# Attention stage of a decoder step: cached products in four stretches, three buffers of probabilities, 128-wide transposes of the new tokens, page numbers read ahead

## The chip, the core and the metric

The kernel runs on one core of a Trainium2 chip (trn2). The core has TensorE (PE in the profile; its weight loads are PEld), VectorE (DVE), ScalarE (ACT), GpSimd (POOL) and SyncE (SP), which in this kernel issues the transfers. The metric is the time of one execution in microseconds on the device, the median of several runs; lower is better.

## The reference

One inference step of a two-layer decoder trunk, for a prompt of 256 tokens and for 8 sequences that each get 8 new tokens after 256 cached ones. The first layer mixes with an mLSTM, the second with attention over shared keys and values; both have a half feed-forward network ahead and behind. What matters here is the attention of the second layer (D 1024, 8 heads of 128):

```python
q = (h @ w_q_b[j]).reshape(bt, t, B_HEADS, B_HD)
att = moba_attention(q, k_all, v_all, q_pos, q_block)
out = att.reshape(bt, t, B_HW) @ w_out_b[j]
...
s = jnp.einsum('bqhd,bqhnkd->bqhnk', qf, kg.astype(F32)) * scale
s = s - slopes[None, None, :, None, None] * dist.astype(F32)
s = jnp.where(ok[..., None] & (dist >= 0), s, -jnp.inf)
p = jax.nn.softmax(s.reshape(bt, q_block, nh, -1), axis=-1).reshape(s.shape)
out = jnp.einsum('bqhnk,bqhnkd->bqhd', p, vg.astype(F32))
```

For the prompt `k_all` and `v_all` are its own 256 tokens. For the 8 sequences they are two pages of 128 cached tokens each, found in a pool by `page_table`, and the 8 new tokens behind them.

## The kernel before

Activations lie transposed, 320 token columns wide (256 of the prompt, 64 new). A product with a weight matrix is a run of "units" of 2 x 8 blocks; each block is three passes (lines 556 to 558) over a high and a low part of weights and activations. ACT and DVE split the raw weights into those parts two units ahead of PE, and SP loads raw weights into a ring of four slots (`raw`). Attention stands between the unit run of the queries (U_Q, four units) and that of the output projection (U_OB, four units).

There is no scheduler: every engine runs a list written out by hand and waits on semaphores. In the attention stage the lists hold these steps (S, T and so on are my short names):

- S(h), `prompt_scores`, lines 954 and 955: scores of head h of the prompt, 128 + 256 columns. DVE adds the position bias and takes maxima (`prompt_bias`, lines 2122 and 2127) into the buffer `pp`, which lies in the room `work`, ACT takes the exponential (`prompt_exp`, line 1538), DVE divides by the sum (`prompt_probs`, lines 2132 and 2134).
- T(h), `prompt_turn`, line 965: three transposes of the probabilities. ACT copies them to `pt` (`prompt_copy`, line 1545).
- O(h), `prompt_outputs`, lines 975 and 976: probabilities times values. ACT and DVE keep the high and low part (`prompt_hi` 1549, `prompt_lo` 2140), which free the output bank for O(h + 1).
- C(b), `cache_scores`, lines 1001 and 1007: for sequence b, the scores of all heads against both cached pages. Each matmul gives 32 rows, and four of them run beside each other in four column groups (form 128*32 in the trace). `new_scores`, line 984, does the same for the new tokens.
- N(i) and P(i), `turn_new_probs` (1018) and `turn_page_probs` (1024): transposes of the probabilities `ss` of four sequences and four heads, for the new tokens and for the two pages. DVE spreads them (`spread_probs`, 2157 to 2162).
- V(b), `cache_outputs`, line 1059: probabilities times cached values, four column groups again; `new_outputs`, line 1037, is the part of the new tokens. Sequences 0 to 3 go to bank 4, 4 to 7 to banks 0 and 2.
- the rows of the sequences are turned in `turn_early_outputs` (1070) and `turn_late_outputs` (1081).

Pages are "cache units": 0 to 7 are the keys of the eight sequences, 8 to 15 their values, each of two pages of 512 KB. Units 4 to 8 and 13 to 15 go to rooms of their own, the others to the ring; the rooms of 13, 14 and 15 are those of the keys 4, 5 and 6, so their loads wait until these keys are used (`kv_used`). For each page SP reads the number from `pages` and then issues the transfer (`page_of`, `load_cache`, `load_room`, lines 493 to 509). Units 7 and up are issued once the last query unit is multiplied.

Of the kernel before, what the change touches and what calls it, by code (L numbers as in the profile page):

```python
# [26 lines left out]
H = 8  # L27
# [42 lines left out]
def trunk_program(nc, w_in, w_out, w_a, w_oa, w_kv, w_q, w_ob, w_gate, xp_in, con_in, row_in,  # L70
# [6 lines left out]
    with ctx:  # L77
# [30 lines left out]
        pp = work[:, 0:768].rearrange("p (s k) -> p s k", s=2)  # L108
        pt = work[:, 768:1536].rearrange("p (s k) -> p s k", s=2)
# [14 lines left out]
        with ExitStack() as ov:  # L124
# [35 lines left out]
            with ExitStack() as own:  # L160
# [6 lines left out]
                ss = sb("ss", [128, 4, PAST + SLOT], f32, own)  # L167
                o_rows = sb("o_rows", [128, 4, DV], f32, own)
                page_k = sb("page_k", [128, 2048], f32, own)
                st = sb("st", [128, 2, 6], f32, own)  # L170
# [226 lines left out]
        def prompt_score_bank(h):  # L397

            return bank[{1: 6, H - 1: 1}.get(h, 5)]
# [31 lines left out]
        def _(sp):  # L431
# [60 lines left out]
            sp.wait_ge(s_pg, 16)  # L492
            def page_of(c, j):

                at = NPG * (c % NB) + j
                page = sp.value_load(pages[0:1, at:at + 1], min_val=0, max_val=kc_in.shape[0] - 1)
                return (kc_in if c < NB else vc_in)[bass.ds(page, 1), :, :].rearrange("a p c -> p (a c)")
# [55 lines left out]
        def _(pe):  # L553
# [404 lines left out]
            def prompt_turn(h):  # L958
# [5 lines left out]
                for i in range(3):  # L964
                    mm = pe.transpose(bank[6][:, i * 128:i * 128 + 128],
                                      pp[:, h % 2, i * 128:i * 128 + 128], ident)
# [46 lines left out]
            def turn_new_probs(i):  # L1013
# [3 lines left out]
                w = SLOT * (r % 2) + SLOT  # L1017
                pe.transpose(bank[r][0:w, 256:384], ss[:, r, PAST + SLOT - w:PAST + SLOT], ident)
# [65 lines left out]
            pe.wait_ge(x_ready, 4 * KT)  # L1084
            prompt_scores(0)
            prompt_scores(1)
            new_scores(0)
# [7 lines left out]
            cache_scores(0, (1,))  # L1095

            def cache_unit(c):

                if c < NB:
                    cache_scores(c)  # L1100
                else:
                    cache_outputs(c - NB)

            cache_unit(1)

            prompt_scores(2)
            prompt_turn(0)
            cache_unit(2)
            cache_unit(3)
            pe.wait_ge(qa_sp, 4)  # L1110
            cache_unit(4)

            prompt_outputs(0)
            prompt_scores(3)
            prompt_turn(1)
            cache_unit(5)
            cache_unit(6)
            cache_unit(7)

            turn_new_probs(0)  # L1120
            turn_page_probs(0)
            prompt_scores(4)
            prompt_turn(2)
            prompt_outputs(1)
            turn_new_probs(1)
            turn_new_probs(2)
            prompt_scores(5)
            turn_page_probs(1)
            turn_page_probs(2)
            prompt_outputs(2)  # L1130
            prompt_turn(3)
# [3 lines left out]

            turn_new_probs(3)
            turn_page_probs(3)
            prompt_outputs(3)
            prompt_turn(4)
            prompt_scores(6)  # L1140
            prompt_scores(7)
            prompt_turn(5)
            prompt_outputs(4)
            new_outputs(1)
            for c in range(NB + 4, NB + 7):
                cache_unit(c)

            prompt_turn(6)
            prompt_outputs(5)
            turn_early_outputs()  # L1150
# [4 lines left out]
            turn_late_outputs(0)  # L1155
            prompt_outputs(7)
            turn_late_outputs(1)
# [49 lines left out]
        def _(sc):  # L1207
# [447 lines left out]
        def _(ve):  # L1655
# [806 lines left out]
```

## Time and profile before

| | |
|---|---|
| median of 3 runs | 1240.37 us (1240.34 to 1240.64) |
| the profiled execution | 1240.44 us |
| its span | 1238.6 us |
| PE busy | 1233.2 us (100%), 8875 matmuls |
| PEld, DVE, ACT, POOL busy | 1210.4, 726.1, 582.7, 81.1 us |
| PE clock granted | 9 in each of 40 slices (90% or more) |
| DMA | 200.39 MB, mean 162 GB/s |
| attention stage | 936.8 to 969.1 us of the span |

The 1.8 us between the profiled time and its span lie outside the instructions and are taken as fixed.
### The profile page before, as it was taken

To read this page: it belongs to the slowest core of one execution; us is meant where nothing else is said; L and a number is where in the kernel's file an instruction comes from. 1 tells how busy PE (TensorE), PEld (TensorE's weight loads), DVE (VectorE), ACT (ScalarE), POOL (GpSimd) and SP (SyncE) were. 2 spreads that over 40 slices of the span, in tenths; PEclk is the share of its full clock that TensorE was granted. 3 is DMA by queue.
4 is the path that set the end of the run, shared out by engine and by line. 5 is a ranking of instruction groups with operands and counts; after the bars stand their busy time and mean duration, and the time that the engine had idled before them with its cause. 6 is when DMAs were issued, how large, how long until landed. Compare 5 with 4: busy or idle time off the path is not lost.

```text
span 1238.6 us, 22056 instructions
## 1 busy us (share of the span) xinstructions
PE 1233.2 (100%) x8875; PEld 1210.4 (98%) x8875; DVE 726.1 (59%) x1127; ACT 582.7 (47%) x936; POOL 81.1 (7%) x99
## 2 busy tenths in 40 slices
PE   9999999999999999999999999999999999999998
PEld 9999999989999999999998999999998999999998
DVE  7656554575777656555564565655467585565443
ACT  6534333464556445443345554534344474544343
POOL 0000000100332000000000000000020110000010
PEclk9999999999999999999999999999999999999999
DMA  8344334543354443334543734334478734433341
GB/s 341 137 161 144 112 132 155 205 147 131 127 164 147 157 166 137 134 121 140 187 166 137 262 136 151 143 105 153 163 277 317 287 139 142 163 135 127 125 156 43
DMA packets 34778, 200.39 MB, mean 162 GB/s; under 512 B 4050, under 2 KB 4186, under 8 KB 19490
## 3 DMA queue, kind: packets, MB, share of 16 engines
q1 hardware_dynamic: 32706, 192.24, 44.0%
q0 software_dynamic: 2016, 7.39, 1.9%
q8 instruction: 38, 0.62, 0.2%
q14 instruction: 18, 0.15, 0.0%
HBM read 193.03 MB, written 6.57 MB: 161 GB/s over the span
## 4 chain that ended last, share of the span: by engine, by line
PE 99%; DMA 0%; SPq 0%; DVE 0%; ACT 0%; issue 0%; DVEq 0%
PE bank L556 30%; PE bank L558 30%; PE bank L557 29%; PE bank L714 1%; PE bank L713 1%; PE bank L712 1%; PE bank L716 1%; PE bank L715 1%; PE bank L1059 1%; DMA xp<-xp_in 0%; PE bank L867 0%; PE bank L822 0%; PE bank L975 0%; PE bank L1001 0%; PE bank L1007 0%; PE bank L955 0%
## 5 line engine op out<-in xcount | busy, mean ns | idle before, releaser
L556 PE MATMUL bank<-h_hi,w_hi 128*128 128x320 f32 x1792 | 555.6, 310 | 0.5 <-DVE h_lo L1682 0.5
L558 PE MATMUL bank<-h_hi,w_lo 128*128 128x320 f32 x1792 | 553.8, 309 | 0.0
L557 PE MATMUL bank<-h_lo,w_hi 128*128 128x320 f32 x1792 | 553.7, 309 | 0.0
L1222 ACT ACTIVATE w_hi<-raw 128x1024 fp32r<-128x1024 f32 (+1 forms) x364 | 331.7, 958 | 440.7 <-PE bank L558 421.7
L1668 DVE TENSOR_TENSOR w_lo<-raw,w_hi 128x1024 fp32r<-128x1024 f32 (+1 forms) x364 | 388.5, 1108 | 133.1 <-ACT w_hi L1222 133.0
L556 PEld LDWEIGHTS bank<-h_hi,w_hi 128*128 128x128 f32 x1792 | 336.3, 188 | 2.6 <-issue 1.4
L557 PEld LDWEIGHTS bank<-h_lo,w_hi 128*128 128x128 f32 x1792 | 336.4, 188 | 0.1
L558 PEld LDWEIGHTS bank<-h_hi,w_lo 128*128 128x128 f32 x1792 | 336.3, 188 | 0.0
L557 PE MATMUL bank<-f_lo,w_hi 128*128 128x320 f32 x704 | 216.5, 308 | 0.0
L558 PE MATMUL bank<-f_hi,w_lo 128*128 128x320 f32 x704 | 216.5, 308 | 0.0
L556 PE MATMUL bank<-f_hi,w_hi 128*128 128x320 f32 x704 | 216.5, 308 | 0.0
L1711 DVE TENSOR_TENSOR work<-bank,rms 128x320 f32<-128x320 f32 x88 | 43.2, 491 | 152.0 <-PE bank L558 151.5
L558 PEld LDWEIGHTS bank<-f_hi,w_lo 128*128 128x128 f32 x704 | 131.9, 187 | 0.0
L556 PEld LDWEIGHTS bank<-f_hi,w_hi 128*128 128x128 f32 x704 | 131.9, 187 | 0.0
L557 PEld LDWEIGHTS bank<-f_lo,w_hi 128*128 128x128 f32 x704 | 131.9, 187 | 0.0
L1272 ACT ACTIVATE f_hi<-work 128x320 f32 (+1 forms) x88 | 41.5, 472 | 124.0 <-DVE work L1719 124.0
L1726 DVE TENSOR_TENSOR f_lo<-work,f_hi 128x320 f32 (+1 forms) x88 | 43.3, 492 | 64.5 <-ACT f_hi L1272 64.5
L2281 POOL TENSOR_TENSOR norm_room<-norm_room 128x320 f32<-128x320 f32 x41 | 43.8, 1068 | 264.9 <-ACT norm_room L1244 263.7
L1731 DVE SCALAR_TENSOR_TENSOR xp<-bank,xp 128x320 f32<-128x320 f32 x31 | 15.3, 493 | 67.3 <-PE bank L558 67.3
L2278 POOL COPY norm_room<-norm_room 128x320 f32<-128x320 f32 x6 | 5.0, 836 | 723.1 <-ACT norm_room L1244 723.1
L1682 DVE SCALAR_TENSOR_TENSOR h_lo<-xp,h_hi 128x320 fp32r<-128x320 f32 x56 | 44.8, 833 | 3.4 <-ACT h_hi L1247 3.4
L1719 DVE TENSOR_TENSOR work<-work 128x320 f32<-128x320 f32 x88 | 42.8, 486 | 4.8 <-ACT work L1268 4.8
(263 smaller groups left out, 763.0 us busy)
## 6 DMA issues: line engine op xcount, KB each, us to landing
raw<-w_in SPq DMA_DIRECT2D x86, 1024.0 KB, 4.8
raw<-w_out SPq DMA_DIRECT2D x64, 704.0 KB, 4.0
raw<-w_a SPq DMA_DIRECT2D x12, 1024.0 KB, 4.7
raw<-w_kv SPq DMA_DIRECT2D x8, 1024.0 KB, 4.7
raw<-w_oa SPq DMA_DIRECT2D x4, 1024.0 KB, 6.0
raw<-w_q SPq DMA_DIRECT2D x4, 1024.0 KB, 4.7
raw<-w_ob SPq DMA_DIRECT2D x4, 1024.0 KB, 11.8
raw<-kc_in SPq DMA_DIRECT2D x8, 512.0 KB, 4.5
```

The costliest lines, as they stand in the source:

```text
L556: pe.matmul(out, wh, mh, start=first, stop=False)
L557: pe.matmul(out, wh, ml, start=False, stop=False)
L558: return pe.matmul(out, wl, mh, start=False, stop=last)
L1222: sc.activation(w_hi[:, n_at % 2, part * w:part * w + w], raw[:, raw_of(n_at) % RAW, part * w:part * w + w], ACT.Copy).then_inc(hi_done, 1)
L1272: sc.activation(dst, up[:, k_at % 2, :], ACT.Copy).then_inc(hid_hi, 1)
L1668: ins = ve.tensor_tensor(w_lo[:, n_at % 2, c], raw[:, raw_of(n_at) % RAW, c], w_hi[:, n_at % 2, c].bitcast(f32), ALU.subtract)
L1682: ve.scalar_tensor_tensor(out=h_lo[:, m, :], in0=x[:, m, :], scalar=par[:, P_G + KT * norm + m:P_G + KT * norm + m + 1], in1=h_hi[:, m, :] ...
L1711: ve.tensor_tensor(gate[:, k_at % 2, :], bank[b][:, 0:T], rms[:, :], ALU.mult).then_inc(gate_ready, 1)
L1719: ve.tensor_tensor(up[:, k_at % 2, :], up[:, k_at % 2, :], act[:, k_at % 2, :], ALU.mult).then_inc(hid_ready, 1)
L1726: ve.tensor_tensor(lo, up[:, k_at % 2, :], hi.bitcast(f32), ALU.subtract).then_inc(hid_lo, 1)
L1731: ve.scalar_tensor_tensor(out=x[:, m, :], in0=bank[4 + m % 2][:, 0:T], scalar=0.5, in1=x[:, m, :], op0=ALU.mult, op1=ALU.add).then_inc(x_r ...
L2281: gp.tensor_tensor(sqsum[:, :], sqsum[:, :], sq[:, m % 2, :], ALU.add).then_inc(sum_done, 1)
```

## The change

The lists of PE, ACT and DVE in the attention stage are written in another order, and four things change beside:

1. The cached products (C and V) stand in four stretches: units 0 to 6; 7, the new tokens' part and 8 to 11; 12 to 14; 15. Prompt steps that stood between them go behind or ahead.
2. `pp` and `st` have three buffers instead of two, in the same room `work`, and the scores of heads 2 and 4 go to bank 4. S(2) is issued at the start; bias and exponential of head h wait for head h - 3 and no longer for h - 2. `new_outputs(0)`, which writes bank 4, waits until head 4 is biased (`pr_b` 5).
3. `turn_new_probs` transposes a full width of 128 instead of 32 or 64. `ss` is wider by 96 columns for that, which POOL sets to zero once, long before.
4. The page numbers of units 7 to 13 are read by `read_pages` during the query units, ahead of units 1, 2 and 3's loads. `page_of` also reads both numbers of any other unit before its first page is issued.

```diff
-        pp = work[:, 0:768].rearrange("p (s k) -> p s k", s=2)
-        pt = work[:, 768:1536].rearrange("p (s k) -> p s k", s=2)
+        pp = work[:, 0:1152].rearrange("p (s k) -> p s k", s=3)
+        pt = work[:, 1152:1920].rearrange("p (s k) -> p s k", s=2)
...
-            return bank[{1: 6, H - 1: 1}.get(h, 5)]
+            return bank[{1: 6, 2: 4, 4: 4, H - 1: 1}.get(h, 5)]
...
+            def read_pages(units):
+
+                for c in units:
+                    for j in range(NPG):
+                        at = NPG * (c % NB) + j
+                        page_read[c, j] = sp.value_load(pages[0:1, at:at + 1], min_val=0,
+                                                        max_val=kc_in.shape[0] - 1)
...
             load_room(6, 1)
+            read_pages((7,))
             load_cache(1)
+            read_pages((NB, NB + 1, NB + 2))
             load_cache(2)
+            read_pages((NB + 3, NB + 4, NB + 5))
             load_cache(3)
...
+            BIASED_BEFORE = {3: 1, 4: 3, 5: 4, 6: 6}
+
             def prompt_scores(h):
-                if 2 <= h < H - 1:
-                    pe.wait_ge(pr_b, h if h > 2 else 1)
+                if h in BIASED_BEFORE:
+                    pe.wait_ge(pr_b, BIASED_BEFORE[h])
...
-                w = SLOT * (r % 2) + SLOT
-                pe.transpose(bank[r][0:w, 256:384], ss[:, r, PAST + SLOT - w:PAST + SLOT], ident)
+                at = PAST - SLOT * (r % 2)
+                pe.transpose(bank[r][:, 256:384], ss[:, r, at:at + 128], ident)
...
                 pe.wait_ge(sm_tc, 6 * q + 6)
+                if q == 0:
+                    pe.wait_ge(pr_b, 5)
...
-                if h >= 2:
-                    sc.wait_ge(pr_p, h - 1)
+                if h >= 3:
+                    sc.wait_ge(pr_p, h - 2)
...
-                if h >= 2:
-                    ve.wait_ge(pr_t, h - 1)
+                if h >= 3:
+                    ve.wait_ge(pr_t, h - 2)
...
+            gp.memset(ss[:, :, PAST + SLOT:PAST + 128], 0.0).then_inc(spread_set, 1)
```

The new list of PE, in the short names, from the first scores on ("new" is `new_scores`, "n-out" `new_outputs`; strokes bound the stretches of four-column-group work):

```
before: S0 S1 | new C0 C1 | S2 T0 | C2 C3 C4 | O0 S3 T1 | C5 C6 C7 | N0 P0 S4 T2 O1 N1 N2 S5 P1 P2 O2 T3 |
        n-out0 V0..V3 | N3 P3 O3 T4 S6 S7 T5 O4 | n-out1 V4 V5 V6 | T6 O5 early | V7 | T7 O6 late0 O7 late1
after:  S0 S1 S2 | new C0..C6 | T0 S3 N0 P0 T1 O0 S4 N1 T2 S5 P1 O1 | C7 n-out0 V0..V3 |
        T3 O2 N2 S6 P2 T4 N3 O3 early P3 S7 T5 O4 | n-out1 V4 V5 V6 | O5 T6 | V7 | T7 O6 late0 late1 O7
```

The new list of DVE after the bias of heads 0, 1 and 2 and the first two `sample_bias` is: probs 2, bias 3, spread 0, lo 0, bias 4, spread 1, bias 5, sample bias 2, probs 3, probs 4, sample bias 3, lo 1, lo 2, spread 2, probs 5, lo 3, spread 3, bias 6, bias 7 and so on; before, it was bias 3, lo 0, probs 2, sample bias 2, probs 3, bias 4, lo 1, spread 0, spread 1, sample bias 3, bias 5, lo 2, probs 4, spread 2, probs 5, spread 3, lo 3, bias 6, bias 7.

First place, PE at the first cached products. Before, the rows from S(1) on (x4 to x16 are matmuls of 32 rows; the first two rows are the scores of head 1):

```order
L954 MATMUL bank<-k_all,qa 128x128
L955 MATMUL bank<-k_all,qa 128x256
L984 MATMUL bank<-k_all,qa 32x32 x8
L1007 MATMUL bank<-raw,q_spread 32x256 x4
L984 MATMUL bank<-k_all,qa 32x32 x8
L1007 MATMUL bank<-raw,q_spread 32x256 x12
L954 MATMUL bank<-k_all,qa 128x128
L955 MATMUL bank<-k_all,qa 128x256
L965 MATMUL bank<-con,work 128x128 x3
L1007 MATMUL bank<-raw,q_spread 32x256 x16
```

After the change (line numbers are those of the changed kernel; the first two rows are S(2)):

```order
L969 MATMUL bank<-k_all,qa 128x128
L970 MATMUL bank<-k_all,qa 128x256
L999 MATMUL bank<-k_all,qa 32x32 x8
L1022 MATMUL bank<-raw,q_spread 32x256 x4
L999 MATMUL bank<-k_all,qa 32x32 x8
L1022 MATMUL bank<-raw,q_spread 32x256 x28
L1016 MATMUL bank<-page_k,q_spread 32x128 x16
L1016 MATMUL bank<-keys_room,q_spread 32x128 x16
L1016 MATMUL bank<-row_room,q_spread 32x128 x4
L1016 MATMUL bank<-norm_room,q_spread 32x128 x4
L1016 MATMUL bank<-row_room,q_spread 32x128 x4
L1016 MATMUL bank<-norm_room,q_spread 32x128 x4
```

The scores of head 2 stand ahead, the turn of head 0 (`bank<-con,work`) is gone from between the products, and key units 4, 5 and 6 (`page_k`, `keys_room`, `row_room` with `norm_room`) follow the ring's units at once.

Second place, PE from the key unit 7 (`split_room<-q_spread`) on. Before:

```order
L1001 MATMUL bank<-split_room,q_spread 32x128 x16
L1018 MATMUL bank<-con,ss 32x128
L1024 MATMUL bank<-con,ss 128x128 x2
L954 MATMUL bank<-k_all,qa 128x128
L955 MATMUL bank<-k_all,qa 128x256
L965 MATMUL bank<-con,work 128x128 x3
L975 MATMUL bank<-work,v_tok 128x256
L976 MATMUL bank<-work,v_tok 128x128
L1018 MATMUL bank<-con,ss 32x128
L1018 MATMUL bank<-con,ss 64x128
```

After:

```order
L991 MATMUL bank<-work,v_tok 128x128
L1016 MATMUL bank<-split_room,q_spread 32x128 x16
L1054 MATMUL bank<-v_tok,p_new 32x128 x8
L1076 MATMUL bank<-split_room,p_spread 32x128 x16
L1076 MATMUL bank<-raw,p_spread 32x128 x48
L980 MATMUL bank<-con,work 128x128 x3
L990 MATMUL bank<-work,v_tok 128x256
```

Unit 7 stood ahead of the first transposes; it now stands next to the new tokens' values (`v_tok,p_new`) and the value units 8 to 11, and the transposes of `ss` come before it.

Third place, SP at the pages of unit 7. Before, from its first transfer on (`TENSOR_LOAD pages` reads a page number, ISA are register instructions):

```order
L509 DMA split_room<-kc_in 128x1024
L496 TENSOR_LOAD pages
L496 ISA x2
L509 ISA
L509 DMA split_room<-kc_in 128x1024
L496 TENSOR_LOAD pages
L496 ISA x2
```

After, from the last reads ahead of unit 3's loads on:

```order
L500 TENSOR_LOAD pages
L500 ISA x2
L500 TENSOR_LOAD pages
L500 ISA x2
L514 ISA
L514 DMA raw<-kc_in 128x1024
L514 ISA
L514 DMA raw<-kc_in 128x1024
L519 ISA
L519 DMA split_room<-kc_in 128x1024
L519 ISA
```

Each transfer of unit 7 and on stood behind a read of its own; now they follow each other, and the reads stand ahead of unit 3.

## Rows read from the trace of the kernel before

**Rows 1.** Timeline of PE: start, duration, line, form; stage's first and last.
```profile
936.80 0.38 PE L954 MATMUL bank<-k_all,qa 128*128 128x128 f32 x2
...
969.08 0.38 PE L556 MATMUL bank<-h_hi,w_hi 128*128 128x320 f32 x1
```

**Rows 2.** The same timeline: steps at edges of stretches and between.
```profile
937.46 0.38 PE L954 MATMUL bank<-k_all,qa 128*128 128x128 f32 x2
...
940.32 0.49 PE L954 MATMUL bank<-k_all,qa 128*128 128x128 f32 x2
...
941.19 0.55 PE L965 MATMUL bank<-con,work 128*128 128x128 f32 x3
941.67 1.93 PE L1007 MATMUL bank<-raw,q_spread 128*32 128x256 f32 x32
...
950.98 0.38 PE L1018 MATMUL bank<-con,ss 128*32 128x128 f32 x2
951.32 0.49 PE L954 MATMUL bank<-k_all,qa 128*128 128x128 f32 x2
...
952.07 0.60 PE L1024 MATMUL bank<-con,ss 128*128 128x128 f32 x4
...
960.31 0.49 PE L965 MATMUL bank<-con,work 128*128 128x128 f32 x3
960.63 0.60 PE L975 MATMUL bank<-work,v_tok 128*128 128x256 f32 x2
...
961.38 0.65 PE L1037 MATMUL bank<-v_tok,p_new 128*32 128x128 f32 x16
...
962.72 1.06 PE L1059 MATMUL bank<-page_k,p_spread 128*32 128x128 f32 x32
963.59 1.06 PE L1059 MATMUL bank<-keys_room,p_spread 128*32 128x128 f32 x32
964.58 0.55 PE L965 MATMUL bank<-con,work 128*128 128x128 f32 x3
```

**Rows 3.** Waits of PE's weight loads, 930 to 985 us (total, times, longest).
```profile
PEld bank L965 <- DVE work L2134: 0.3, 1, 0.3
```

**Rows 4.** Timeline of SP's queue: transfers issued (units 1, 3, 7, 15; w_ob).
```profile
922.75 0.34 SPq L504 DMA_DIRECT2D raw<-kc_in  x1
...
935.32 0.34 SPq L504 DMA_DIRECT2D raw<-kc_in  x1
...
937.71 1.44 SPq L509 DMA_DIRECT2D split_room<-kc_in  x2
...
957.33 0.34 SPq L509 DMA_DIRECT2D norm_room<-vc_in  x1
...
957.71 0.91 SPq L443 DMA_DIRECT2D raw<-w_ob  x2
```

**Rows 5.** DMA issues at 935.32, 937.71 and 957.33: KB, us to landing.
```profile
raw<-kc_in SPq DMA_DIRECT2D x1, 512.0 KB, 5.0
...
split_room<-kc_in SPq DMA_DIRECT2D x1, 512.0 KB, 4.6
...
norm_room<-vc_in SPq DMA_DIRECT2D x1, 512.0 KB, 8.4
```

**Rows 6.** Busy time in a window (PE, PEld, DVE, ACT, POOL), clock, DMA, GB/s.
```profile
950.00:955.00 5.00, 5.00 (x77) 4.40 (x79) 4.86 (x20) 3.03 (x11) 0.00 (x0) 1.00 1.03 415
```

**Rows 7.** Timeline of PE: start of the last cached product, V(7).
```profile
965.93 0.43 PE L1059 MATMUL bank<-row_room,p_spread 128*32 128x128 f32 x8
```

**Rows 8.** Timeline of DVE: bias of head 3, spread 2, lo 3.
```profile
946.42 0.56 DVE L2122 SCALAR_TENSOR_TENSOR work<-con,bank 128x384 f32<-128x384 f32 x1 [0.84 <-PE bank L965]
...
956.45 0.48 DVE L2157 COPY p_spread<-bank 128x128 f32<-128x128 f32 x2
...
959.28 0.42 DVE L2140 TENSOR_TENSOR h_lo<-bank,h_hi 128x256 fp32r<-128x256 f32 x1
```

More of the change, by code:

```diff
@@ L492, in _ @@
             sp.wait_ge(s_pg, 16)
+            page_read = {}
+            def read_pages(units):
[4 more added lines that the diff above has]
+                                                        max_val=kc_in.shape[0] - 1)
             def page_of(c, j):
-                at = NPG * (c % NB) + j
-                page = sp.value_load(pages[0:1, at:at + 1], min_val=0, max_val=kc_in.shape[0] - 1)
-                return (kc_in if c < NB else vc_in)[bass.ds(page, 1), :, :].rearrange("a p c -> p (a c)")
+                if (c, j) not in page_read:
+                    read_pages((c,))
+                return (kc_in if c < NB else vc_in)[bass.ds(page_read[c, j], 1), :, :].rearrange("a p c -> p (a c)")
             def load_cache(c):
@@ L1084, in _, with cache_unit @@
             pe.wait_ge(x_ready, 4 * KT)
+            def cache_unit(c):
+                if c < NB:
+                    cache_scores(c)
+                else:
+                    cache_outputs(c - NB)
             prompt_scores(0)
             prompt_scores(1)
+            prompt_scores(2)
             new_scores(0)
@@ L1095, in _ @@
             cache_scores(0, (1,))
[L1097 to L1106, printed above, removed]
-            prompt_turn(0)
[L1108 to L1113, printed above, removed]
+            for c in range(1, 4):
+                cache_unit(c)
+            pe.wait_ge(qa_sp, 4)
+            for c in range(4, 7):
+                cache_unit(c)
+            prompt_turn(0)
             prompt_scores(3)
[L1115 to L1118, printed above, removed]
             turn_new_probs(0)
             turn_page_probs(0)
+            prompt_turn(1)
+            prompt_outputs(0)
             prompt_scores(4)
+            turn_new_probs(1)
             prompt_turn(2)
-            prompt_outputs(1)
-            turn_new_probs(1)
-            turn_new_probs(2)
             prompt_scores(5)
             turn_page_probs(1)
-            turn_page_probs(2)
-            prompt_outputs(2)
-            prompt_turn(3)
+            prompt_outputs(1)
+            cache_unit(7)
             new_outputs(0)
@@ L1134, in _ @@
                 cache_unit(c)
+            prompt_turn(3)
+            prompt_outputs(2)
+            turn_new_probs(2)
+            prompt_scores(6)
+            turn_page_probs(2)
+            prompt_turn(4)
             turn_new_probs(3)
+            prompt_outputs(3)
+            turn_early_outputs()
             turn_page_probs(3)
-            prompt_outputs(3)
-            prompt_turn(4)
-            prompt_scores(6)
             prompt_scores(7)
@@ L1553, in sample_exp @@
                 sc.wait_ge(sm_m, i + 1)
-                sc.activation(ss[:, r, :], ss[:, r, :], ACT.Exp, bias=sst[:, 0, r:r + 1],
+                sc.activation(ss[:, r, 0:PAST + SLOT], ss[:, r, 0:PAST + SLOT], ACT.Exp, bias=sst[:, 0, r:r + 1],
                               accum_out=sst[:, 1, r:r + 1]).then_inc(sm_e, 1)
@@ L1570, in late_hi @@
                               ACT.Copy).then_inc(sm_hi, 1)
-            prompt_exp(0)
-            prompt_exp(1)
-            prompt_copy(0)
-            prompt_exp(2)
+            for h in range(3):
+                prompt_exp(h)
             sample_exp(0)
             sample_exp(1)
+            prompt_copy(0)
+            prompt_copy(1)
             prompt_hi(0)
             prompt_exp(3)
-            prompt_copy(1)
-            sample_exp(2)
+            prompt_exp(4)
             prompt_hi(1)
             prompt_copy(2)
-            prompt_hi(2)
-            prompt_copy(3)
-            prompt_exp(4)
+            sample_exp(2)
             sample_exp(3)
-            prompt_exp(5)
-            prompt_hi(3)
-            prompt_copy(4)
             sc.wait_ge(kv_used, NB + 4)
@@ L1593, in _ @@
             sample_rows(0, bank[4][:, 0:DV])
+            prompt_copy(3)
+            prompt_hi(2)
             sample_rows(2, bank[4][:, DV:2 * DV])
+            prompt_exp(5)
+            prompt_copy(4)
+            prompt_hi(3)
+            early_hi()
+            prompt_hi(4)
+            prompt_copy(5)
             prompt_exp(6)
-            prompt_hi(4)
             prompt_exp(7)
-            prompt_copy(5)
+            prompt_hi(5)
             prompt_copy(6)
-            early_hi()
-            prompt_hi(5)
             sc.wait_ge(sm_og, 1)
@@ L1606, in _ @@
             late_hi(0)
+            prompt_hi(6)
             late_hi(1)
-            prompt_hi(6)
             prompt_hi(7)
```

51 lines of the change are left out of this document (25 added, 26 removed).

## Prediction

> **What bounds the kernel now.** I first read the busy shares on the page: PE is busy for 1233.2 of 1238.6 us, so nothing that DVE, ACT or SP saves counts by itself; only what shortens PE's own list, or a wait of PE, does. The change touches PE's list in the attention stage alone, so I went to PE's timeline there. The first scores start at 936.80 and the first pass of the output projection at 969.08 [rows 1]: the stage takes 32.28 us, 2.6% of the time. The whole can only move by what moves in it. Then the waits of PE in the stage: only one that another engine causes is above 0.2 us, T0 behind DVE's probabilities [rows 3]. So the stage is not held up by waits; what it holds beside its bare products is the edges between kinds of work.
>
> Bare steps, from start to start [rows 1, 2]: S takes 0.66 (936.80 to 937.46), and O, with the same 384 columns, the same; T takes 0.32 (960.31 to 960.63); a cached product V 0.87 (962.72 to 963.59). A transpose of 128 columns is a third of a T, 0.11. With 8 S, 8 O, 8 T, 16 C or V, 16 single transposes (N, P, early, late) and some 1.2 for the new tokens' parts, the bare sum is 10.6 + 2.6 + 13.9 + 1.8 + 1.2 = 30.1. The stage has 2.2 us over that, and no reordering of it can give back more: 0.18% of 1240. Below I count changes within 0.2% (2.5 us), about what a measurement of this kernel can tell from no change, as the same.
>
> Second in line is the stream of pages. Over 950 to 955 the DMA engines are full (share 1.03, 415 GB/s) at a granted clock of 1.00 [rows 6], the upper one of PE's levels, 2.4 GHz. The last page is issued at 957.33 and lands 8.4 later, at 965.73 [rows 4, 5]; V7, which needs it, starts at 965.93 [rows 7]. So the stream ends 0.2 us ahead of its use: whatever PE saves ahead of V7 is lost there unless the pages come earlier too. This decides what the reordering is worth.
>
> **The change part by part.**
>
> *Two stretches fewer.* I count six stretches of four-column-group work before and four after (the change's own words say seven). An edge costs, on entering: O4 takes 0.75 (960.63 to 961.38) instead of 0.66, so 0.09. On leaving: V6 takes 0.99 (963.59 to 964.58) instead of 0.87, so 0.12, and leaving C1 is dearer: S2 behind it takes 0.87 (940.32 to 941.19) instead of 0.66, with T0's wait at its end. T0 ahead of C2 takes 0.48 (941.19 to 941.67) instead of 0.32, 0.16 [rows 2]. For two stretches I take the mean of entering, 0.12, and 0.17 for leaving: 2 x 0.29 = 0.58, from 0.42 (both at the low rows) to 0.7.
> By the Trainium skill, TensorEngine Tiling (Array Packing), Tiling Modes, a change of the tiling mode drains the array, and TensorE: Matmul & The Clock Gate gives that drain as 128 cycles, which is 0.053 us at 2.4 GHz: by that, four edges would give 0.21, an estimate; the rows of this trace say more than twice that.
>
> *128-wide transposes.* N1 and N2 take 0.34 together (950.98 to 951.32) instead of 0.22, and S5 behind them 0.75 (951.32 to 952.07) instead of 0.66 [rows 2]: they are edges of the same kind, 0.21 in sum. N0 stands beside a stretch and N3 alone; I count nothing for them. In the new order all are full width between full-width steps: 0.21 saved. The wider `ss` costs POOL one memset during the query units, where it has nothing else to do, and DVE and ACT still touch 288 columns.
>
> *T0's wait.* T0 is issued some 4 us later, when the probabilities are long there; 0.10 saved of the 0.3 that the weight load waited [rows 3] (S2's and T0's rows leave no more beside their edges).
>
> *The end.* Before, late0, O7, late1; now late0, late1, O7. The same 0.77 us of work covers the way from late0 over ACT and DVE to the first pass. Nothing.
>
> Sum: 0.58 + 0.21 + 0.10 = 0.89 us, if no wait comes in. To see which may, I lay PE's new list out with the bare steps and edges above, from 936.80: three S to 938.78, new tokens and C0 to 940.02 (their length before, 1.15, and 0.09), C1, C2, C3 (from 941.77) to C6 and its edge, 945.38; T0, S3, N0, P0, T1, O0, S4, N1, T2, S5, P1, O1 to 950.36; C7 from 950.46, new tokens 0.46, V0, V1, V2, V3 (from 954.44) to 955.43; T3 0.38, O2 (from 955.81), N2, S6, P2 (to 957.46), T4, N3, O3, early, P3, S7, T5, O4 to 960.73; new tokens' outputs (from 960.73), V4 to V6 to 963.93; O5, T6, V7 from 965.07; T7, O6, late0, late1, O7 and the hand-over to the first pass at 968.19, which is 969.08 less 0.89. Against that:
>
> *Pages read ahead.* Two issues with a read between them are 1.10 apart (two in 1.44, of which the second takes 0.34), two of `w_ob` without one 0.91 - 0.43 = 0.48 [rows 4]: a read costs some 0.62. It goes from the pages of unit 7 and on, where it spaced issues by 1.10 us while a page needs 0.524 MB / 415 GB/s = 1.27 us on the engines [rows 6], to the time ahead of units 2 and 3. (a) Unit 7's first page is issued at about 937.0 instead of 937.71. It would land at 941.6 to 942.6 (4.6 later [rows 5], or 1 us more behind unit 3's pages, which now come late). 17 pages follow. At 1.27 each the last lands at 963.2; at the pace of before, (965.73 - 942.31) / 17 = 1.38, from the later start, at 966.0. V7 wants it at 965.07: a wait of 0 to 0.9. V3's last page is eight earlier, 953.0 to 955.8, and wanted at 954.44: 0 to 1.4. SP no longer spaces them, and the queue stays full, so I take the quicker pace and 0.3 us of wait. The ring's slots are free in time: C0 to C3 are done by 942.7, earlier pages keep the engines busy until then. (b) Unit 3: after unit 1's second issue (922.75 [rows 4]) SP makes 6 + 2 reads, two issues, 6 + 2 reads: 16 x 0.62 and three spacings put unit 3's second page at about 934.9, at 0.76 a read (1.10 - 0.34) at 936.4, instead of 935.32. With 5.0 to land [rows 5] that is 941.4 at worst; C3 wants it at 941.77. Free by 0.4 us.
>
> *Three buffers, DVE's list.* DVE's bias of head 3 started at 946.42 and spread 2 at 956.45 [rows 8]: 10.03 us for bias 3 to 5, lo 0 to 2, probs 2 to 4, two sample biases, spread 0 and 1. In the new list bias 3 waits for S3 (done 946.4), and the same steps without lo 2 (0.42 [rows 8]) and probs 2 stand ahead of O2's release (lo 1): lo 1 is done at about 955.4 counting 0.6 for probs 2, and O2 wants it at 955.81. Then n-out 1: spread 2 starts after P2 at 957.6; spread 2, probs 5, spread 3 took 959.28 - 956.45 = 2.83 [rows 8], with lo 3 between them 3.2: 960.8, less 0.2 for the last reciprocal, 960.6, against 960.73. Free by 0.4 and 0.1, so I count nothing, but it is tight. The third buffer itself saves PE nothing where it did not wait; it lets DVE start bias 2 without T0.
>
> Forecast: 1240.44 (the profiled execution, 0.07 above the median of 1240.37) - 0.89 + 0.3 = 1239.85; against the median, 1239.8.
>
> **The rivals.**
> 1. *The page stream keeps its landings.* V3 waits, V7 starts at 965.93 as before, and only what stands behind it could change, which is nothing: 1240.4. For it: full engines [rows 6], a landing only 0.2 ahead of V7 [rows 5, 7]. Against it: the start is 0.7 earlier, and 1.38 a page before is slower than the engines' 1.27. Chance 0.2. The Trainium skill, DMA: Bandwidth & Descriptors, gives about 358 GB/s as the limit of one core's HBM traffic: 1.46 us a page, by which the last page would land at 966.4 and the time be 1240.9, an estimate; the 415 of this trace speaks against it.
> 2. *Unit 3 comes late.* If eight more reads delay it by over 1.4 us, PE stands at C3; a further 0.8 us eats the gain: 1240.4 from then on. For it: the reads stand in its way, and all pages of units 3 and 7 are now within 2 us. Against: 0.4 us free at the dearest read. Chance 0.08.
> 3. *DVE hands over too late, and the kernel is slower.* From 946.4 on DVE has no idle time until lo 1 and again until spread 3. Each us that it slips beyond 0.4 (O2) or 0.1 (n-out 1) is PE's. From 0.7 us of slip at n-out 1 on the change is a loss; at a slip of 2 us (14% of the 14 us from 946.4) it gives 1240.44 - 0.59 + 1.9 = 1241.8, and only at 3.2 a loss of over 0.2%. Against it: the same instructions with the same operands, timed by rows. Chance 0.1.
> 4. *No wait at all:* 1240.37 - 0.89 = 1239.5 or, with edges at their dear rows, 1239.3; part of the forecast's own range.
>
> **How the numbers follow.** The forecast (1239.3 to 1240.3) has 0.62, rivals 1 to 3 0.2, 0.08 and 0.1. The range must hold 8 in 10: below, 1239.1, since more than 1.2 us would need waits that I do not see; above, past 1240.4 and half of rival 3, 1241.0. Faster by over 0.2% needs 1237.9 or less, more than the 2.2 us in the stage: 0.03, for a change outside it. Slower by over 0.2%, 1242.9 or more, is the far end of rival 3 and what I overlook: 0.05. The rest, 0.92, is the same.
>
> **What would show it.** Right: first pass of the projection about 0.6 us after 968.2; C6's end near 945.4; no edge at N1 and N2; issues of unit 7's pages 0.35 to 0.5 apart from 937.0; last page at 963 to 965. Wrong: a wait of PE ahead of `raw<-vc_in` products or at V7 (rival 1), at C3 (rival 2), at O2 or `v_tok,p_new` (rival 3). It would be wrong altogether if the passes outside the stage changed their pace.

## The result, and the profile after

The changed kernel takes 1242.41 us (17 runs, 1241.24 to 1244.06) against 1240.38 (17 runs, 1239.96 to 1240.88) of the kernel before: a ratio of 1.0018, interval 1.0011 to 1.0024. It is slower, by 0.16% between the medians, which is within the 0.2% that the prediction counts as the same, but 2.6 us above the forecast and outside its range. The profiled execution took 1242.41 with a span of 1240.6.

PE's timeline of the changed kernel (start, duration, line, form; in brackets the idle time and its releaser), at the places of [rows 1, 2, 7]:

```profile
936.99 0.38 PE L969 MATMUL bank<-k_all,qa 128*128 128x128 f32 x2
...
945.51 0.55 PE L980 MATMUL bank<-con,work 128*128 128x128 f32 x3
...
951.48 0.62 PE L1054 MATMUL bank<-v_tok,p_new 128*32 128x128 f32 x16
951.92 1.06 PE L1076 MATMUL bank<-split_room,p_spread 128*32 128x128 f32 x32
952.79 2.47 PE L1076 MATMUL bank<-raw,p_spread 128*32 128x128 f32 x70
957.06 1.06 PE L1076 MATMUL bank<-raw,p_spread 128*32 128x128 f32 x26 [1.80 <-issue]
958.05 0.55 PE L980 MATMUL bank<-con,work 128*128 128x128 f32 x3
...
965.50 0.73 PE L1076 MATMUL bank<-page_k,p_spread 128*32 128x128 f32 x17 [0.22 <-issue]
...
968.33 0.43 PE L1076 MATMUL bank<-row_room,p_spread 128*32 128x128 f32 x8
...
971.43 0.38 PE L569 MATMUL bank<-h_hi,w_hi 128*128 128x320 f32 x1
```

The stage now takes 971.43 - 936.99 = 34.44 us, 2.16 more than before [rows 1]. Up to V1 it keeps the layout of the prediction: T0 was laid out at 945.38 and V0 at 951.8 or so, and with the start 0.19 later they come at 945.51 and 951.92. Then V3 is torn: its first 6 products are the last of the row of 70 that begins with V1, and its other 26 come only from 957.06. The waits of the same stretch (total, times, longest):

```profile
PEld bank L1076 <- issue: 2.7, 3, 2.1
...
PE bank L1076 <- issue: 2.0, 2, 1.8
...
PEld bank L1076 <- DMA raw<-vc_in: 0.4, 1, 0.4
```

The page wait of the forecast is there, 0.4 us ahead of V3. The larger wait is put down to "issue": PE stood for 2.07 us (from the last product's start, 954.99, to 957.06; the brackets count from its end), inside a unit whose data had all landed, and no semaphore released it. DVE and ACT were not what was missing; DVE itself stood still for 4.35 us, until the high part of O2, which PE had not yet multiplied.

The stream came nearly as laid out: unit 7's pages were issued from 937.32 on (laid out for 937.0), 0.52 apart, and the last page, issued at 950.36, landed 14.6 us later, at 965.0, in the 963 to 965 that the prediction gave (KB, us to landing):

```profile
norm_room<-vc_in SPq DMA_DIRECT2D x1, 512.0 KB, 14.6
```

What the time between 955 and 957 has beside it is one line in the list of DMA queues on the page, of which I had made nothing:

```profile
q8 instruction: 38, 0.62, 0.2%
```

38 packets of 16 KB. They are not data. That they are PE's program is taken from what follows: such a packet starts 2.2 to 2.6 us ahead of the end of every gap in this document. In windows of the changed kernel (PE and PEld busy with their counts, clock, DMA share, GB/s) I counted PE's weight loads from the first scores on:

```profile
936.80:955.60 18.80, 18.34 (x392) 15.29 (x390) 16.45 (x55) 9.26 (x33) 0.00 (x0) 1.00 0.99 389
...
936.80:951.16 14.36, 14.36 (x263) 11.84 (x265) 12.43 (x42) 7.54 (x28) 0.00 (x0) 1.00 0.98 382
...
955.60:965.20 9.60, 8.14 (x125) 7.29 (x125) 5.06 (x18) 4.91 (x17) 0.00 (x0) 1.00 1.03 413
```

The first gap stands behind 390 loads, the second 125 loads later (a window also counts one or two loads that only end in it, so single counts are good to that, and differences are better), and 125 loads with their 125 matmuls and a few waits are about 256 instructions. So 16 KB of PE's program end where PE stands; the border before the first gap (load 265) was crossed at 951.2. The Trainium skill, Runtime: NRT & Kernel Launch, Instruction fetch mechanics, gives the same size, blocks of 16 KiB or 256 instructions, and says of the crossing that it is "mostly hidden". The size agrees, the second half does not: 2.07 and 0.49 us stand bare here. In narrow windows of the queues (packets, MB, share) the packet is in 954.6 to 954.8, 3.5 us behind that crossing, and PE goes on 2.4 us later:

```profile
q8 instruction: 1, 0.02, 34.6%
```

In the kernel before the same border was crossed at 950.87, its packet started at 953.1, 2.2 later (at the borders beside it, crossed at 944.1, 956.5 and 963.0, it was 2.7 to 3.1), and PE needed 5.6 us for the block, to 956.45, since T3 and O2 stood between the transposes and the value units:

```profile
950.87:956.45 5.58, 5.58 (x125) 5.03 (x126) 5.44 (x22) 3.84 (x14) 0.00 (x0) 1.00 1.03 414
```

After the change the block holds hardly anything but products of 128 columns on four column groups. Without its waits it is through in some 3.4 us. The theory at this point (the expectations call it block theory): a block is asked for when the border one ahead is crossed, its packet comes late where the DMA engines are full, PE has it 2.2 to 2.6 us after the packet's start, and what the block before takes less than the sum of both is a gap.

### The profile page after: what moved, and what is told of

It reads as the page before. It is cut to its first block, busy times and chain, and to the rows that moved or that the text cites. A ratio compares the mean times of both kernels' runs of the same rounds, so it can differ in the third digit from the quotient of the medians.

```text
span 1240.6 us, 22056 instructions
## 1 busy us (share of the span) xinstructions
PE 1233.5 (99%) x8875; PEld 1211.4 (98%) x8875; DVE 726.4 (59%) x1127; ACT 583.4 (47%) x936; POOL 81.5 (7%) x100
## 4 chain that ended last, share of the span: by engine, by line
PE 98%; DMA 1%; SPq 0%; issue 0%; DVE 0%; ACT 0%; DVEq 0%
PE bank L569 30%; PE bank L571 29%; PE bank L570 29%; PE bank L727 1%; PE bank L726 1%; PE bank L725 1%; DMA raw<-vc_in 1%; PE bank L729 1%; PE bank L728 1%; PE bank L1076 0%; PE bank L880 0%; DMA raw<-w_in 0%; PE bank L835 0%; PE bank L856 0%; PE bank L990 0%
```

## The experiments

Times are medians beside the kernel before on the same chip, which had 1240.4 to 1240.5. Gaps, waits and packets are read from each one's trace.

**e1: the changed kernel with the page numbers read as before; e2: the kernel before with the numbers read ahead; e3: the changed kernel, pages of unit c issued only when unit c - 2 has landed.**

```
e1  -            read_pages((7,))                      (and the two others; each number is read
    -            read_pages((NB, NB + 1, NB + 2))       ahead of its issue again)
e2  +            read_pages((7,)) ...                  (all three, in before)
e3  +                landed(c - 2)                     (waits on unit c - 2's loads)
```

> The changed kernel with page numbers read one by one as before; all orders and buffers of the change kept. Queue theory (PE's program comes in blocks of 16 KB over the same DMA engines, and pages issued earlier make these blocks late): the 2.07 us gap inside V3 shrinks to under 0.5 us; V3's page lands at about 955 and V7 is held by its page until about 966, so 1240.0 to 1240.8. Density theory (the four-column-group products stand in longer runs and use up the program faster than blocks come, whatever the pages do): a gap of some 2 us stays in V2 or V3, 1242 to 1243. Page theory (the wait for V3's page alone): 1242 or more, since its page comes later than now.

> The kernel before with the page numbers read ahead as in the change, nothing else. Queue theory: gaps without a semaphore wait appear inside the cached products, 1241 to 1243. Density theory: PE's list is that of before, so no gap, 1240.2 to 1240.5 (pages come earlier, nobody waited for them).

> The changed kernel, but SP issues the pages of unit c (9 and up) only once unit c - 2 has landed, so at most six pages queue. Queue theory: with 10 to 13 us of queue cut to 5 or so, no gap over 0.5 us in the products, V7 near 965.5: 1239.4 to 1240.2, the gain that was forecast. Density theory: a gap of about 2 us in V2 or V3 stays, 1242 or more. Both expect up to 0.5 us of waits for pages, since the engines may run dry for a moment between units.

e1 took 1242.12 (1.0016, 1.0007 to 1.0025). V3 now waited longer for its page, and the rest of the block's delay was hidden in that wait:

```profile
955.41 0.42 PE L1063 MATMUL bank<-raw,p_spread 128*32 128x128 f32 x6 [1.05 <-DMA raw<-vc_in]
956.15 1.06 PE L1063 MATMUL bank<-raw,p_spread 128*32 128x128 f32 x26 [0.32 <-issue]
```

The gap, 0.59 us from start to start, is behind the same 390 loads, and its packet started 3.0 us behind the crossing. The stage took 33.62. e2 took 1240.39 (1.0001, 0.9992 to 1.001), stage 32.28 as before, no gap. e3 took 1242.93 (1.0021, 1.0012 to 1.003):

```profile
954.68 0.42 PE L1084 MATMUL bank<-raw,p_spread 128*32 128x128 f32 x6 [0.38 <-DMA raw<-vc_in]
956.25 1.06 PE L1084 MATMUL bank<-raw,p_spread 128*32 128x128 f32 x26 [1.16 <-issue]
...
965.43 1.08 PE L1084 MATMUL bank<-keys_room,p_spread 128*32 128x128 f32 x32 [0.50 <-DMA keys_room<-vc_in]
...
968.60 0.43 PE L1084 MATMUL bank<-row_room,p_spread 128*32 128x128 f32 x8 [0.91 <-DMA norm_room<-vc_in]
```

What follows: reading ahead is neither the gain nor the loss. The depth of the queue is not the cause: pages issued at 947 to 951 took 11.4 to 12.0 us to land in e2 and its packet was 2.2 behind the crossing; 4.2 us in e3, and its packet was 3.3 behind.

**e4: the changed kernel with the transposes of the new tokens 32 and 64 wide again.**

```
-                pe.transpose(bank[r][:, 256:384], ss[:, r, at:at + 128], ident)
+                pe.transpose(bank[r][0:w, 256:384], ss[:, r, PAST + SLOT - w:PAST + SLOT], ident)
```

> The changed kernel with the new tokens' transposes 32 or 64 wide again. Step of the prediction: edges of 0.1 us at N0, N1, N2 and N3 come back, the stage's list is 0.4 to 0.9 us longer (twice or more of the 0.21 that the change was credited with, as all four stand alone now); the time 1242.5 to 1243.5 if the gap stays as it is. Rival: the width costs nothing, time as the changed kernel.

1242.18 (1.0019, 1.001 to 1.0028). From T0 to C7 it takes 5.07 us (945.23 to 950.30), exactly as the changed kernel does (945.51 to 950.58), with narrow transposes between:

```profile
945.23 0.55 PE L980 MATMUL bank<-con,work 128*128 128x128 f32 x3
...
948.24 0.27 PE L1033 MATMUL bank<-con,ss 128*32 128x128 f32 x1
948.35 0.49 PE L980 MATMUL bank<-con,work 128*128 128x128 f32 x3
...
950.30 1.08 PE L1016 MATMUL bank<-split_room,q_spread 128*32 128x128 f32 x32
```

The second half of the list agrees: from T3 to the new tokens' outputs both take 5.29 us (957.66 to 962.95, and 958.05 to 963.34). The width is worth nothing. The gap stayed, 2.29 us behind 390 loads.

**e5: the changed kernel with 96 more instructions of PE ahead of the stage, waits on a semaphore long reached; e6: the kernel before with 192 of them.**

```
+                for _ in range(idle[0]):          # 4 (e5) or 8 (e6) ahead of each k-tile
+                    pe.wait_ge(ones_set, 1)       # of query units 1 to 3
```

> The changed kernel with 96 more instructions on PE during the query units (waits that are long fulfilled), so that each border between 16 KB blocks of PE's program (256 instructions) falls 48 loads earlier in the attention list; nothing else moves. Block theory (PE stands where it reaches a border while the next block, asked for at the border before, is still on its way over the full DMA engines, some 5 to 6 us): the block that lay in C7 to V3 and lasted 3.8 us is now spread over 6.4 us, so the 2.07 us gap in V3 is gone; the block from about 961 to 966 lasts 4.7 us and may cost up to 1.2. 1239.7 to 1241.0. Rival (the gap belongs to V3 and its pages, not to a place in the program): gap in V3 stays, 1242 or more.

> The kernel before with 192 such waits more: a border moves to the start of V0 and the next to the end of V3, 256 instructions that last 3.4 us. Block theory: a gap of 1.5 to 2.3 us near the end of V3 without any change to orders, buffers or pages: 1241.9 to 1242.8. Rival (the gap comes from the changed lists): 1240.2 to 1240.6, no gap.

e5 took 1241.98 (1.0013, 1.0004 to 1.0022). The gaps moved, as two rows of PE and two windows show:

```profile
954.85 2.37 PE L1082 MATMUL bank<-raw,p_spread 128*32 128x128 f32 x74 [1.21 <-issue]
...
968.49 0.30 PE L1082 MATMUL bank<-row_room,p_spread 128*32 128x128 f32 x1 [0.82 <-issue]
```

```profile
936.70:954.00 17.30, 16.93 (x344) 14.08 (x342) 15.21 (x52) 8.71 (x31) 0.00 (x0) 1.00 1.00 388
954.00:968.00 14.00, 12.82 (x252) 11.47 (x252) 9.13 (x32) 7.96 (x26) 0.00 (x0) 1.00 1.03 414
```

342 loads instead of 390: 48 pairs earlier, which is 96 instructions, and the next gap two times 126 loads on. V3 has no gap any more; the border lies in V1 now, and the gap with it. The time is outside the 1239.7 to 1241.0 that the block theory gave: the block ahead of the gap lasted 6.4 us (crossed at 947.0, at its end at 953.4), as laid out, and PE still stood for 1.49 us, since the packet came only at 952.5, 5.5 us behind its crossing. So the place of a gap follows the theory and its size does not. e6 took 1244.79 (1.0035, 1.0023 to 1.0047): the kernel before, whose order and data are untouched, gets gaps of its own, 2.13 us behind 423 loads and 1.06 us another 126 loads later. This shows that the place of the gaps is a count of instructions, and that the kernel before was only lucky in where its borders fall and in what stands around them. The time is above the 1241.9 to 1242.8 that was expected for one gap: there are two, and the profiled execution also lost clock. Behind the first gap the granted clock was 0.61 in the mean of 4.4 us (0.50, the lower level of 1.2 GHz, from 961 to 964), and the steps there last twice as long:

```profile
960.00:964.40 4.40, 4.40 (x23) 3.86 (x20) 2.18 (x8) 1.39 (x4) 0.00 (x0) 0.61 1.03 412
```

What the clock costs e6 is not told apart: four of its six runs had a mean clock of 1.000 and took 1244.38 to 1245.00 all the same.

**e7: the changed kernel with the value unit 8 alone loaded and read by all eight value units (the value pages of units 9 to 15 are left out); e8: e7, and the loads of `w_ob` and `w_in` held until the seventh value unit is done.**

```
e7  -            for c in range(NB + 1, CACHE): ...    (no loads of value units 9 to 15)
    +                room = ROOM[NB]                   (V0 to V7 all read it)
e8  +            sp.wait_ge(kv_used, NB + 7)           (ahead of w_ob[1] to w_ob[3])
```

> The changed kernel without the 14 value pages of units 9 to 15: all V steps read the room of unit 8, so the rows of the sequences are not those of the reference; instructions and their order stay. The DMA engines are nearly idle from 946 to about 953. Block theory with the engines' load in it: the block asked for at C7 comes within 2 us, no gap in V3, 1239.3 to 1240.2. Rival (a block takes as long on idle engines, only the density of instructions counts): the gap of about 2 us stays.

> The changed kernel with two kinds of loads taken out of the stretch: as in e7 only the value unit 8 is loaded and all value units read it (the value pages of units 9 to 15 are left out), and SP issues the loads of w_ob and w_in only when the seventh value unit is done. In e7 the w_ob and w_in packets kept the 16 engines full to 954, and the instruction packet of TensorE started at 954.77, just as they ran empty. Here they have nothing to carry from about 946 on. Load theory: the packet waits for the DMA engines. With them idle it starts at most 1 us behind the crossing of the border before it (at 951.2), TensorE has its instructions by 954.6, and there is no gap at the border (0 to 0.3) or in V5; the first pass of the projection starts 2.0 to 2.6 us earlier against the stage's start than in e7, before what the later w_ob loads cost behind it (the whole kernel may well be slower by some us for these late loads, so the stage is read and not the time). Dispatch theory: the packet is late because TensorE takes 250 instructions in 3.8 us, whatever the DMA engines do: the packet starts at 954 to 955 as before and the gap stays at 2.0 to 2.6 us.

In e7 the freed queue took the weight loads at once, so that the engines were still nearly full (share 0.94) to 954.7. It took 1241.91 (1.0016, 1.0007 to 1.0025) with the largest gap of all, 2.57 us, though no unit waited for a page; the expectation, no gap with engines that are idle, could not be tested by it:

```profile
957.04 1.06 PE L1069 MATMUL bank<-split_room,p_spread 128*32 128x128 f32 x26 [2.29 <-issue]
```

In e8 the engines are idle from 946 to 963. It took 1239.35 (0.999, 0.9981 to 1.0), and there is no gap at all; PE's rows, then two windows of it:

```profile
936.96 0.38 PE L963 MATMUL bank<-k_all,qa 128*128 128x128 f32 x2
...
951.88 3.68 PE L1070 MATMUL bank<-split_room,p_spread 128*32 128x128 f32 x128
955.49 0.55 PE L974 MATMUL bank<-con,work 128*128 128x128 f32 x3
...
968.26 0.38 PE L563 MATMUL bank<-h_hi,w_hi 128*128 128x320 f32 x1
```

```profile
936.70:951.13 14.43, 14.43 (x264) 11.91 (x267) 12.44 (x42) 7.55 (x28) 0.00 (x0) 1.00 0.53 205
951.13:954.52 3.39, 3.39 (x135) 3.39 (x129) 3.22 (x12) 1.16 (x4) 0.00 (x0) 1.00 0.02 5
```

The block is run through in 3.39 us, faster than in any other kernel, and its successor is there: the packets start 0.7 us (951.8) and 0.8 us (955.3) behind the crossings (951.13, 954.52). PE's list and its borders are those of e7; only the loads differ. So at this border it is the full DMA engines that make the packet late, and not the density of PE's list. The stage of e8 takes 31.30 us, 0.98 less than before: this is what the change saves without page wait and gaps (V0 to V7 read one unit, but they are the same products).

**e10: the changed kernel, PE waits for unit 11's last page already ahead of V0.**

```
+                if b == 0:
+                    last = raw_of_cache(NB + 3)
+                    pe.wait_ge(loaded[last % RAW], loads_after(last))
```

> The changed kernel in which TensorE waits for the last page of unit 11 already ahead of V0 (the unit itself runs in V3), so that it stands still from 951.9 to 954.8 instead of 0.4 us ahead of V3 and 2.07 us inside it. Block theory: the next 16 KB of its program come 2.4 us behind their packet, at 957.0 or a little later, however TensorE spends the time up to the border; from V0 it reaches the border 2.7 us after its start, at 957.5, and finds them there: no gap or up to 0.3 us, V3's end at 958.4 to 958.7 against 958.05, so the wait of 2.9 us costs only 0.4 to 0.6 us, time 1242.3 to 1243.0. Rival, the gap comes from the length of the run of products (352 instructions at 73 a us) and not from the time since the last border: it stays at about 2 us behind the wait, V3's end at 960.4 to 960.7, time about 1244.8.

1243.13 (1.0023, 1.0014 to 1.0033). In the profile PE stands 2.57 us ahead of V0 and then runs through V3 and its border without a gap:

```profile
954.27 1.08 PE L1079 MATMUL bank<-split_room,p_spread 128*32 128x128 f32 x32 [2.29 <-DMA raw<-vc_in]
955.17 2.80 PE L1079 MATMUL bank<-raw,p_spread 128*32 128x128 f32 x96
```

A wait that I put in took the place of the gap, and the profiled stage is 33.80 us, not longer than the 34.44 of the changed kernel. So the gap is time since the last border, not something in V3. (The median did not follow the profiled stage down: the five runs with a mean granted clock of 1.000 took 1241.76 to 1242.40, the five with less 1243.86 to 1244.44.)

**e11: the changed kernel, the pages of units 13 to 15 issued only when V3 is done; all data are loaded.**

```
+                if c == NB + 5:
+                    sp.wait_ge(kv_used, NB + 4)
```

> The changed kernel in which SP issues the pages of the value units 13 to 15 (and the w_ob loads behind them) only when V3 is done, at about 958, so that the 16 engines run dry from about 957, when unit 12 has landed, until then. All data are loaded. The first gap lies ahead of that and stays as it was, about 2.0 us at 955.0, since unit 11's page lands at 954.8 only if the engines are full to there. The second gap, 0.49 in V5 (border crossed at 957.05, packet at 962.99), should by the load theory be gone, since its packet finds idle engines and starts at 957 to 958.5; V7 0.3 to 0.5 earlier against V3's end, first pass at 970.9 to 971.1 if the held pages come in time (V5 is wanted at 964.7; five us from an issue at 958 to an idle queue make 963), time about 1242.0. If the packet waits for something else than the loads, the gap in V5 stays at 0.4 to 0.6. Rival: the held pages are late for V6 or V7 and the time is 1243 or more.

1243.59 (1.0027, 1.0015 to 1.0039). The first gap stayed, 1.72 us. The second was gone, but V6 waited for its page, which is the rival that the expectation named:

```profile
966.99 1.08 PE L1078 MATMUL bank<-keys_room,p_spread 128*32 128x128 f32 x32 [1.38 <-DMA keys_room<-vc_in]
```

And the packet did not come early, as the theory wanted: it started at 962.6, 5.7 behind the crossing of 956.9, although the engines had nothing to do from 957 to 959. e7 shows the same in small: crossing at 957.04, engines at rest, packet at 960.2, 3.2 behind. At the next border of e7, with no gap ahead of it and the engines still at rest, it was 0.2 (964.9, packet at 965.1). So full engines are not the only thing that makes a packet late: behind a gap it is late without them, and I don't know by what rule.

**e9: the kernel before with the wide transposes and the reading ahead alone (`read_pages` as in e2); e12: the changed kernel with all eight key units in one stretch and T3, N2, P2, O2 ahead of the new tokens' outputs, the lists of DVE and ACT to match.** Both were meant to beat both kernels.

```
e9   +                pe.transpose(bank[r][:, 256:384], ss[:, r, at:at + 128], ident)
e12  -            for c in range(4, 7):         +            for c in range(4, 8):
     +            turn_new_probs(2)
     +            turn_page_probs(2)
     +            prompt_turn(3)
     +            prompt_outputs(2)
                  new_outputs(0)
```

> The kernel before with the transposes of the new tokens' probabilities 128 wide (and the memset that they need) and the page numbers read ahead, but with its own seven stretches of cached products and two rooms of probabilities. TensorE's program has the same number of instructions in the same order, so its 256-instruction borders stay where they are, with about 1 us to spare at 956.45. Sum of the prediction's terms: 0.21 us less, time 1240.1 to 1240.3, no gap without a semaphore in the stage. Rival: the wide transposes bring the border forward by 0.2 and something of it is given back, time 1240.3 to 1240.5. This is the only version of those tried that could beat both kernels by more than 0.1 us.

> A version that could beat both. From the changed kernel: all eight key units in one stretch (unit 7 directly behind unit 6), and T3, N2, P2 and O2 moved ahead of the first new tokens' outputs, so that the same set of steps stands ahead of them as in the kernel before and the value units come about when they came there; DVE's and ACT's orders follow (sample_bias of row 2 ahead of the bias of head 3, probabilities and low part of the heads 3 and 1 ahead of the bias of head 5). Between the first scores and V0 it has two stretches fewer than before. The block of TensorE's program that ends inside the value run then takes about 5.2 to 5.6 us again. Theory: no gap at the border in V3, or one under 0.6 us; V3's page (954.8) is no wait, as V3 is wanted at about 955.8; stage 31.5 to 31.9 us against 32.28 before and 34.44 after, time 1239.7 to 1240.1. Rivals: DVE, which is busy nearly all the time from 946 to 954, makes T3 or O2 wait 0.5 to 1 us, and the time is that of before (1240.3 to 1240.8); or the block is a little too short and the gap is 1 us or more, time 1241 or more.

e9 took 1240.58 (1.0001, 0.9992 to 1.001), stage 32.30. N1, N2 take 0.29 and S5 0.76 with full width, against 0.34 and 0.75 with 32 and 64 columns [rows 2]:

```profile
951.09 0.38 PE L1031 MATMUL bank<-con,ss 128*128 128x128 f32 x2
951.38 0.49 PE L967 MATMUL bank<-k_all,qa 128*128 128x128 f32 x2
952.14 0.60 PE L1037 MATMUL bank<-con,ss 128*128 128x128 f32 x4
```

e12 took 1243.18 (1.0025, 1.0016 to 1.0035), stage 36.62:

```profile
952.33 0.55 PE L980 MATMUL bank<-con,work 128*128 128x128 f32 x3 [0.63 <-DVE work L2148]
...
959.07 1.29 PE L1076 MATMUL bank<-raw,p_spread 128*32 128x128 f32 x37 [2.14 <-issue]
960.29 0.57 PE L969 MATMUL bank<-k_all,qa 128*128 128x128 f32 x2
```

```profile
960.30:963.60 3.30, 3.30 (x14) 2.83 (x13) 0.00 (x0) 1.12 (x3) 0.00 (x0) 0.54 1.04 418
```

Both rivals came at once. T3 waited for DVE, and the gap was there, 2.41 us, although the block (crossed at 949.9) had by then lasted 6.75 us: this packet came 6.6 us behind its crossing. The length of the block that is needed is therefore no fixed figure, as e5 had shown already. Behind the gap the clock fell to 0.54.

## Why the prediction was wrong, point by point

**The step that failed** is the layout ("To see which may, I lay PE's new list out"). It let PE stand only for pages and for DVE. It has no term for PE's own program, and nearly the whole miss of 2.6 us comes from that. Against e8 with the same list and no wait, T3 comes 2.53 us later after the start (21.06 against 18.53): 0.38 for the page, 2.07 for the block, the rest in starting up twice. Between there and the first pass of the projection another 0.61 is lost, 0.49 of it the second gap. -0.98 + 2.53 + 0.61 = 2.16, which is what the stage lost; the time lost 2.0.

**The sum without waits**, 0.89, was right in size: e8 measured 0.98. Its parts were not. *128-wide transposes*, 0.21: nothing, by e4 and e9. The 0.34 and 0.75 that I took for edges of width are there with wide transposes too; what they are is open. In the new order they are gone with either width. So the new order itself is worth about 0.98, not 0.58 + 0.10; which edge gives how much was not tried alone.

**Page wait**, 0.3: measured 0.38, at V3, whose page landed at 954.8 (laid out for 953.0 to 955.8, wanted at 954.44). The upper end mixes two paces: at 1.38 a page throughout it is 942.6 + 9 x 1.38 = 955.0, and the wait 0 to 0.6 and not 0 to 1.4. The quicker pace was near enough; V7 had no page to wait for, since it came three us late itself.

**Rival 1** (the landings stay) did not happen. **Rival 2**: C3 had no wait. **Rival 3** has the right sign and size of time (1241.8) by the wrong mechanism: DVE was late for nothing. The sentence that it would be "wrong altogether if the passes outside the stage changed their pace" did not bite. What would have shown the risk ahead is in the trace before: the packets of q8, the full engines of [rows 6], and a block of 5.6 us with about 1 us to spare.

**The scatter.** The times of the changed kernel spread over 2.8 us, those of before over 0.9. Of its 17 runs the nine with a mean granted clock of 1.000 took 1241.24 to 1242.49, the eight with 0.998 or 0.999 took 1242.15 to 1244.06, seven of them 1243.0 or more. e4, e10 and e12 part in the same way: with 1.000 they end at 1242.29, 1242.40 and 1243.26, with less they begin at 1243.44, 1243.86 and 1244.58. In e1, e3 and e7 the two kinds overlap. The profiled execution of e12 is one of the longer ones (1244.63), and it has the stretch at the lower clock behind its gap. That the longer ones of the 17 are made in this way is likely and not shown: no profile of one was taken, and in the kernel before the runs below 1.000 that were taken beside the experiments are hardly longer than the others (1240.06 to 1241.29 against 1239.80 to 1241.05).

**What stays open:** with the engines equally full, why the packet comes 2.2 us behind the crossing in the kernel before, 3.0 to 3.8 in the changed one and most of its variants, 5.5 in e5 and 6.6 in e12, while in e6 one came 1.3 behind (946.8, packet at 948.0, engines' share 1.08); and why it is late after a gap when they are idle (e7, e11). No version tried beats the kernel before with all its data loaded.

## What to carry to other kernels

In a straight program on one core with the DMA engines full, look for the instruction queue in the list of queues and for "issue" gaps inside a run of equal matmuls; if they repeat after 125 or so loads, they are program blocks. When a change packs small matmuls into one long run, count how long 256 instructions of PE's list take: with 2.2 to 3.8 us to the packet and 2.4 behind it, a block of under 4.6 to 6.2 us was at risk here, and in e5 and e12 not even 6.4 and 6.75 were enough. To test it, put satisfied waits ahead of the place: if the gap moves by their number, it is the program.

## What the runs showed of the hardware that I had not expected

- A packet of PE's program is a customer of the DMA engines: 0.2 to 0.8 us behind the crossing with idle engines (e8, and e7 at its later border; 3.2 behind the gap of e7), 1.3 to 6.9 with full ones (both ends in e6, the upper one behind its gap), and PE has it some 2.4 us after its start (2.2 to 2.6).
- Instructions that cost PE next to nothing where they stand (192 satisfied waits; the first scores at 936.98 instead of 936.80) made an untouched kernel 4.4 us slower 20 us later.
- A stop of 2.1 to 2.4 us was followed by a stretch at the lower clock in two of the profiled executions (0.61 and 0.54), and in those with gaps of 1.7 to 2.6 us of e4, e7, e11 and the changed kernel it was not.
